# A fused two-block transformer kernel on one core: mLSTM decay matrices made during the value projection, and the first two column groups of five layer norms worked side by side

## What is computed

```
b = jnp.cumsum(lf, axis=-1)
g = b[..., -1]
a = g[..., None] - b + ic
m_loc = a.max(axis=-1)
...
dmat = b[..., :, None] - b[..., None, :] + ic[..., None, :]
dmat = jnp.where(causal, dmat, -jnp.inf)
inter = b + m_prev[..., None]
m_t = jnp.maximum(inter, dmat.max(axis=-1))
sw = jnp.exp(dmat - m_t[..., None]) * jnp.einsum('bhntk,bhnsk->bhnts', qc, kc)
s_inter = jnp.exp(inter - m_t)
```

## Time and profile before

| | us |
|---|---|
| median of 3 runs | 3019.35 (3017.84 to 3020.52) |
| profiled execution, its own time | 3024.82 |
| its span in the profile | 3023.0 |
| PE busy | 2951.9 (98%) |
| POOL busy | 2002.3 (66%) |
| DVE busy | 1487.2 (49%) |
| ACT busy | 679.4 (22%) |

### The profile page before, as it was taken

One profiled execution on the slowest core, in us unless ns is written; L12 is line 12 of the kernel. 1 busy time (PEld: TensorE's weight loads), 2 busy tenths in 40 slices (PEclk: granted clock), 3 DMA queues, 4 the chain that ended last, 5 costly groups with the idle time before them and its releaser, 6 DMA issues.

```text
span 3023.0 us, 37894 instructions
## 1 busy us (share of the span) xinstructions
PE 2951.9 (98%) x13886; PEld 2406.6 (80%) x13886; DVE 1487.2 (49%) x2621; ACT 679.4 (22%) x1500; POOL 2002.3 (66%) x2041
## 2 busy tenths in 40 slices
PE   8999999999999998999999999999999999999998
PEld 6877777788888887777888888778878888888886
DVE  7678784533324777876443322565421221324543
ACT  3265344200001336445110000000111111211000
POOL 6765455877777776444777777787766556565775
PEclk9999999999999999999999999999999999999999
DMA  4322222433334322222333333333333223222332
GB/s 145 98 85 63 64 64 73 129 96 95 94 95 127 95 90 80 58 66 66 123 92 96 97 96 99 91 91 102 97 90 105 77 84 98 84 84 77 95 96 74
DMA packets 86922, 274.37 MB, mean 91 GB/s; under 512 B 10368, under 2 KB 11008, under 8 KB 86784
## 3 DMA queue, kind: packets, MB, share of 16 engines
q1 hardware_dynamic: 85248, 270.44, 29.5%
q10 hardware_dynamic: 1536, 2.10, 0.3%
HBM read 266.21 MB, written 4.19 MB: 89 GB/s over the span
## 4 chain that ended last, share of the span: by engine, by line
PE 90%; DVE 7%; ACT 2%; issue 1%; POOL 0%; DMA 0%; DVEq 0%; SPq 0%; ACTq 0%; POOLq 0%
PE PS L498 60%; PE PS L549 14%; PE PS L778 5%; PE PS L786 3%; PE PS L824 1%; PE PS L836 1%; PE PS L1082 1%; PE PS L865 1%; PE PS L511 1%; PE PS L848 1%; PE PS L1057 0%; PE PS L1069 0%; PE PS L1054 0%; PE PS L763 0%; ACT TB L1184 0%
## 5 line engine op out<-in xcount | busy, mean ns | idle before, releaser
L468 POOL TENSOR_TENSOR WL<-RAW,WH 128x512 fp32r<-128x512 f32 (+2 forms) x538 | 798.5, 1484 | 9.8
L460 POOL TENSOR_TENSOR POOL_C<-POOL_C 128x1 f32<-128x1 f32 x538 | 126.0, 234 | 952.2 <-PE PS L498 540.8
L498 PE MATMUL PS<-XNH,WH 128*128 128x512 f32 x1752 | 692.1, 395 | 3.1 <-DVE OQK L2288 1.6
L498 PE MATMUL PS<-XNL,WH 128*128 128x512 f32 x1752 | 682.6, 390 | 0.0
L465 POOL TENSOR_TENSOR WL<-RAW,WH 128x512 fp32r<-128x512 f32 x420 | 583.5, 1389 | 35.0
L461 POOL TENSOR_SCALAR WH<-RAW 128x1024 fp32r<-128x1024 f32 (+3 forms) x538 | 533.1, 991 | 0.5 <-issue 0.5
L498 PE MATMUL PS<-XNH,WL 128*128 128x512 f32 x1752 | 433.2, 389 | 0.1
L498 PEld LDWEIGHTS PS<-XNH,WH 128*128 128x128 f32 x1752 | 328.4, 187 | 75.9 <-issue 8.2
L498 PEld LDWEIGHTS PS<-XNL,WH 128*128 128x128 f32 x1752 | 328.4, 187 | 70.7 <-issue 3.1
L498 PEld LDWEIGHTS PS<-XNH,WL 128*128 128x128 f32 x1752 | 328.0, 187 | 70.1 <-POOL WL L468 1.2
L549 PE MATMUL PS<-WH,XNH 128*128 128x512 f32 x704 | 279.3, 397 | 1.9 <-issue 1.7
(11 more groups left out here) (371 smaller groups left out, 4433.3 us busy)
## 6 DMA issues: line engine op xcount, KB each, us to landing
RAW<-w_oslot SPq DMA_DIRECT2D x56, 512.0 KB, 3.6
RAW<-w_L0ffn SPq DMA_DIRECT2D x44, 512.0 KB, 3.6
RAW<-w_L1ffn SPq DMA_DIRECT2D x44, 512.0 KB, 3.6
RAW<-w_od SPq DMA_DIRECT2D x32, 512.0 KB, 3.6
RAW<-w_L0G SPq DMA_DIRECT2D x24, 512.0 KB, 3.6
RAW<-w_L1G SPq DMA_DIRECT2D x24, 512.0 KB, 3.6
RAW<-w_epg SPq DMA_DIRECT2D x16, 512.0 KB, 3.7
RAW<-w_eug SPq DMA_DIRECT2D x16, 512.0 KB, 3.6
```

The costliest lines, as they stand in the source:

```text
L460: nc.gpsimd.tensor_tensor(POOL_C[:, 1:2], POOL_C[:, 0:1], POOL_C[:, 0:1], ALU.add)
L468: nc.gpsimd.tensor_tensor(WL[:, half, at_:w], RAW[:, slot, at_:w], WH[:, half, at_:w].bitcast(F32), ALU.subtract).then_inc(S("weights_spli ...
L498: mm = nc.tensor.matmul(bank, w[:, slot, k * cols:(k + 1) * cols], x[:, k0 + k, :], start=first and j == 0 and w is WH and x is hi, stop=l ...
```

## The change

Two things are changed, and a few orders with them.

**mLSTM.** The running sums of the gates are made in the middle of dq (`chunk_sums`, bank 4), and the four spreads during mv: before its second, third and fourth chunk and behind it, into four banks of their own. Four tiles take the place of the one `DM` (`DMS`: `DM`, an eighth of `X`, `SQA` and `DG`). VectorE does the four row maxima in a row, and the small arithmetic once for all chunks where the state doesn't force steps; it stands ahead of the low part of ckv and of the dq norms. ScalarE takes all exponentials in one go ahead of the output gate. The loop over chunks loses `maxima`, the diagonals, the exponentials and the spreads. In it, the key norm of chunk n-1 moves from the end of step n-1 to step n, behind the weighted scores. In the second layer VectorE waits for the saving of `X` to memory, since one of the tiles lies there.

**Layer norms.** At v = 1 to 5 `opening_pair` does the first two chunks together: groups k = 0 to 6 of the one and then of the other, k = 7 of both, the token sums, the low part of the first, the root's spread, the low part of the second. The residual ahead of v = 1, 3 and 5 uses other banks, and `claim` asks at these places only for banks that the next step uses. In `add_residual` `low_part` goes ahead of `add_square`.

```diff
+        DMS = (DM, X[:, 7, :], SQA[:, :], DG)
+        SPREAD_BANKS = (6, 7, 0, 5)
...
+            def opening_pair(v, banks, c, sums, roots):
+
+                def high(half, k):
+                    pe.wait_ge(S("xn_ready"), 8 * v + k + 1)
+                    for x in (XNH, XNL):
+                        nc.tensor.matmul(PS[banks[half]][:, :], WH[:, (c + half) % 2, k * P:(k + 1) * P],
+                                         x[:, k, :], start=k == 0 and x is XNH, stop=False)
+
+                for half in range(2):
+                    claim(banks[half])
+                    pe.wait_ge(S("high_ready"), c + half + 1)
+                    for k in range(KD - 1):
+                        high(half, k)
+                for half in range(2):
+                    high(half, KD - 1)
+                sum_tokens(v, sums)
+                for half in range(2):
+                    pe.wait_ge(S("weights_split"), c + half + 1)
+                    for k in range(KD):
+                        mm = nc.tensor.matmul(PS[banks[half]][:, :], WL[:, (c + half) % 2, k * P:(k + 1) * P],
+                                              XNH[:, k, :], start=False, stop=k == KD - 1)
+                    mm.then_inc(S("chunk_done"), 1)
+                    if half == 0:
+                        spread_roots(v, roots)
...
+                def spread_u(n):
+
+                    b = SPREAD_BANKS[n]
+                    claim(b)
+                    pe.wait_ge(*L("diag_ready", 4 * n + 4))
+                    nc.tensor.matmul(PS[b][:, :], ONES[:, :], DG, start=True, stop=True
+                                     ).then_inc(L("ub_ready"), 1)
+                    release[b] = L("ub_taken", n + 1)
...
+                def in_dq(q):
+                    if q == 2:
+                        chunk_sums()
+
+                def in_mv(q):
+                    if q:
+                        spread_u(q - 1)
...
+                spread_u(3)
...
-                token_group(f"L{li}mo", (1, 2, 3, 4), halfway=lambda: spread_u(0))
+                token_group(f"L{li}mo", (1, 2, 3, 4))
...
-                    if n < NT - 1:
-                        spread_u(n + 1)
...
-                residual(f"L{li}wout", 2 * li, (0, 1), [(KD, 0)], MH, ML, order=LATE_FIRST,
+                residual(f"L{li}wout", 2 * li, (2, 3), [(KD, 0)], MH, ML, order=LATE_FIRST,
...
-                            first_columns(2 * li + 1, PS[0][:, :], c, s)
-                            sum_tokens(2 * li + 1, 4)
+                            opening_pair(2 * li + 1, (0, 1), c, 4, 5)
+                            claim(2, 3)
...
+                act.wait_ge(*L("u_ready", 1))
+                diagonal(0)
                 chunk(seg("dq") + 4)
                 for n, b in enumerate((5, 6, 7, 0)):
                     run(DQR[:, n, :], PS[b][:, :], ACT.Copy, L("dq_raw"), scale=RTOK[:, n:n + 1])
+                for n in range(1, NT):
+                    diagonal(n)
...
+                act.wait_ge(*L("darg_ready", 1))
+                run(ARG, ARG, ACT.Exp, L("pex_ready"))
+                for n in range(NT):
+                    for h in range(M_HEADS):
+                        x = DMS[n][:, h * P:(h + 1) * P]
+                        run(x, x, ACT.Exp, L("pex_ready"), bias=RMAX[:, 4 * n + h:4 * n + h + 1])
...
+                    if v < 6:
+                        low_part(v, k)
                     if k > 1:
                         add_square(v, k - 1)
-                    if v < 6:
-                        low_part(v, k)
...
+                sq_tables = rope_tables(row("sq_g"), 1)
+                norm_tile(TA, 0, RSH, sq_tables, "sq")
                 dve.wait_ge(*L("bg_ready", 1))
...
+                for n in range(1, NT):
+                    norm_tile(TA, n, RSH, sq_tables, "sq")
+                if li:
+                    dve.wait_ge(S("x_saved"), 16 * KD)
+                for n in range(NT):
+                    h4 = slice(4 * n, 4 * n + 4)
+                    ub = heads(PS[SPREAD_BANKS[n]][:, :], 4)
+                    dve.wait_ge(*L("ub_ready", n + 1))
+                    V.tensor_reduce(MAXU[:, h4], ub, AX.X, ALU.max)
+                    V.tensor_tensor(heads(DMS[n], 4), ub, over(CAUSAL[:, 3 * P:], 4), ALU.add
+                                    ).then_inc(L("ub_taken"), 1)
+                    dve.wait_ge(*L("ub_taken", n + 1))
+                    ins = V.tensor_reduce(RMAX[:, h4], heads(DMS[n], 4), AX.X, ALU.max)
+                then(ins)
+                then(V.tensor_tensor(MLOC, G, MAXU, ALU.add))
+                for n in range(NT):
+                    h4 = slice(4 * n, 4 * n + 4)
+                    then(V.tensor_tensor(GM[:, h4], G[:, h4], MPREV[:, h4], ALU.add))
+                    then(V.tensor_tensor(MPREV[:, 4 * n + 4:4 * n + 8], GM[:, h4], MLOC[:, h4], ALU.max))
...
+                then(V.tensor_tensor(MX, MPREV[:, 0:16], RMAX, ALU.max))
+                V.tensor_tensor(w_loc, chunked(U), chunked(MAXU), ALU.subtract)
...
+                V.tensor_scalar(RMAX, MX, -1.0, 0.0, ALU.mult, ALU.add).then_inc(L("darg_ready"), 1)
...
                     if n:
                         total(n - 1)
-                        maxima(n)
                         state(n - 1)
```

More of the change, by code:

```diff
@@ L501, in by_columns @@
                 mm.then_inc(S("chunk_done"), 1)
-            def first_columns(v, bank, c, slot):
-                for w, xs in ((WH, (XNH, XNL)), (WL, (XNH,))):
-                    pe.wait_ge(S("high_ready" if w is WH else "weights_split"), c + 1)
-                    for k in range(KD):
-                        if w is WH:
-                            pe.wait_ge(S("xn_ready"), 8 * v + k + 1)
-                        for x in xs:
-                            mm = nc.tensor.matmul(bank, w[:, slot, k * P:(k + 1) * P], x[:, k, :],
-                                                  start=k == 0 and w is WH and x is XNH,
-                                                  stop=k == KD - 1 and w is WL)
-                mm.then_inc(S("chunk_done"), 1)
             def first_pair(v, banks, c):
@@ L552, in by_tokens, with token_group @@
                 mm.then_inc(S("chunk_done"), 1)
-            def token_group(name, banks, cols=T, k_per=2, n_k=KD, hi=XNH, lo=XNL, at=0, halfway=None):
+            def token_group(name, banks, cols=T, k_per=2, n_k=KD, hi=XNH, lo=XNL, at=0, between=None):
                 for q in range(n_k // k_per):
-                    if halfway is not None and 4 * q * k_per == 3 * n_k:
-                        halfway()
+                    if between is not None:
+                        between(q)
                     c = FIRST[name] + at + q
@@ L612, in layer @@
                         sum_tokens(2 * li, 6)
-                    if j == (1 if li else 2):
+                    if j == 2 and not li:
                         spread_roots(2 * li, 7)
@@ L627, in turn_small, with chunk_sums @@
                     release[4] = L("small_ready", 4)
-                for name, banks, sem in (("ckvq", (5, 6, 7, 0), "ckvq_raw"), ("sq", (1, 2, 3, 4), "sq_raw"),
-                                         ("dq", (5, 6, 7, 0), "dq_raw"), ("mv", (1, 2, 3, 4), "v_ready")):
-                    token_group(f"L{li}{name}", banks, halfway=turn_small if name == "ckvq" else None)
+                def chunk_sums():
+                    claim(4)
+                    pe.wait_ge(*L("lf_ready", 1))
+                    nc.tensor.matmul(PS[4][:, 0:16], TRI[:, :], LF, start=True, stop=True)
+                    nc.tensor.matmul(PS[4][:, 16:32], ONES[:, :], LF, start=True, stop=True
+                                     ).then_inc(L("bg_ready"), 1)
+                    release[4] = L("bg_taken", 1)
@@ new lines, in in_mv @@
+                def in_mv(q):
+                    if q:
+                        spread_u(q - 1)
+                for name, banks, sem, between in (("ckvq", (5, 6, 7, 0), "ckvq_raw", in_ckvq),
+                                                  ("sq", (1, 2, 3, 4), "sq_raw", None),
+                                                  ("dq", (5, 6, 7, 0), "dq_raw", in_dq),
+                                                  ("mv", (1, 2, 3, 4), "v_ready", in_mv)):
+                    token_group(f"L{li}{name}", banks, between=between)
@@ L1040, in _ @@
                 release[b0] = release[b0 + 1] = release[b0 + 2] = (S("ey_ready"), 8 + j + 1)
-            residual("eout", 4, (3, 7), [(KD, 0), (KD, 8)], EYH, EYL, ready=lambda k: (S("ey_ready"), k + 1))
-            claim(0, 1, 2, 3, 4, 5, 6, 7)
+            residual("eout", 4, (3, 5), [(KD, 0), (KD, 8)], EYH, EYL, ready=lambda k: (S("ey_ready"), k + 1))
+            claim(0, 1, 2, 4)
             def scores(s, n):
@@ L1118, in _ @@
                     c, b = FIRST[f"oslot{s}"] + q, 6 + (7 * s + q) % 2
-                    if s == 0 and q == 0:
-                        first_columns(5, PS[b][:, :], c, c % 2)
-                        sum_tokens(5, 4)
+                    if s == 0 and q < 2:
+                        if q == 0:
```

(8 more changed lines are left out.)

138 lines of the change are left out of this document (49 added, 89 removed).

## The result

| | before | after |
|---|---|---|
| median | 3019.93 us (3017.84 to 3023.21, 4 runs) | 2999.85 us (2998.97 to 3000.49, 4 runs) |
| profiled execution, its own time | 3024.82 | 2999.98 |
| its span | 3023.0 | 2998.2 |

The ratio is 0.9933, with a 95% interval of 0.992 to 0.9945: a gain of 20.1 us, where 31.6 was forecast and 2982 to 2998 was the range. The time is 11.9 us above the 2988 that was said. From profile to profile the gain is 24.8 us.

What follows compares the result with a forecast made beforehand. TensorE, busy 98% of 3023.0 us, plus its standstills was taken as the bound. Terms 17.6 + 5.1 + 1.5 + 9.4 - 2.0 = 31.6 us off 3019.35 gave 2987.8, said as 2988, range 2982 to 2998.

Steps and rivals of the forecast that it cites:

- the low clock is not in the plain runs: Rival, 15 in 100: plain runs lack the half-clock stretches, so only 26.5 us go, giving 2993 us.
- turning of the weighted scores: mLSTM loop: TensorE's waits for VectorE's product all go once the maxima leave the loop, 17.6 us.
- half-clock stretches in the loops: mLSTM loops: three stretches at the 1.2 GHz level behind TensorE's long waits go with them, 5.1 us.
- L738, L719: mLSTM loop: TensorE's waits for ScalarE go as diagonals and exponentials leave the loop; 1.5 us taken of 2.2.
- norms: Layer norms: waits for low parts, last X and the evacuation needing the root all go, 9.4 us.
- ScalarE late at the output gate: Behind mv: ScalarE's exponentials may delay the output gate; 1 us charged per layer, 2.0 together, ends 0 and 8.
- the first rival: Rival, 17 in 100: VectorE becomes the mLSTM loop's bound, held up by GpSimd; 10 us back, 2998 us.
- The 16 small operations behind mv: VectorE's small arithmetic after the last maxima, behind mv: 2.4 to 10.9 us, 6.7 taken.
- mv without a wait: During mv: the moved spreads and ScalarE's diagonals make TensorE wait nowhere, so nothing was charged.
- the product's time: Loop step 3, layer 0: VectorE's product is done by about 232.2, 2.1 us before TensorE gets there.
- The ladder: Rival, 3 in 100: in mv, diagonals and spreads wait on each other; new waits from 33.6 us make it slower.
- the empty norms: Rival, 3 in 100: at the layer norms the wait only moves, 9.4 us stay, giving 2997 us.

Runs made afterwards that it cites:

- the norm part alone: Kernel before with only the layer-norm part of the change: 3011.73 us, ratio 0.9969.
- the mLSTM part alone: Changed kernel without its layer-norm part: 3010.59 us, ratio 0.9968.
- without the subtractions: Kernel before, with GpSimd writing zeros as the low parts of the dk weights in place of subtracting: 3010.74 us, ratio 0.9967.
- the dk copies first: Changed kernel with ScalarE's copies of the second pair of dk tiles ahead of its last hidden tile: 3003.86 us, ratio 0.9947.
- the second profile of the kernel before: Kernel before, unchanged, run again: profiled execution 3022.49 us, median 3022.00 us in 12 runs.

## Why the prediction was wrong

In two steps of about equal weight: from the sum's own 2987.8 the time is 12.1 us away, 5.3 by the base and 6.8 by what is late next.

**The base: 5.3 us.** The sum was made against the profiled execution, and then "the same difference off it", 5.5 us, was taken. For the changed kernel this difference is 0.1. The removed wait was also much of what made the kernel scatter: the norm part alone, which leaves the wait in, still lies within 6.3 us (6 executions), the mLSTM part alone, which takes it out, within 2.6 (6 executions). So a gain read from one high execution is too large for the median. The rival that named this ("the low clock is not in the plain runs") had the amount, 5 us, and a reason that holds at most in part: some 3.6 of the 5.1 us are in the average plain execution, by the estimate above.

**What is late next: 6.8 us, 31.6 forecast against 24.8 from profile to profile.** By the terms:

| term | forecast | profiles |
|---|---|---|
| turning of the weighted scores | 17.6 | 17.6 |
| half-clock stretches in the loops | 5.1 | 5.1, all gone |
| L738, L719 | 1.5 | 2.2 |
| norms | 9.4 | 9.4 (alone in the median: 9.0) |
| ScalarE late at the output gate | -2.0 | 0 |
| L836, L778, not foreseen | 0 | 2.0 (1.2 and 0.8) |
| new waits: L539 6.8, L602 2.7 and 1.5 more, L729 0.5 more | 0 | -11.5 |
| sum | 31.6 | 24.8 |

The second row has its check in PE's busy time: L710, L719, L729 and L738 had 5.9 + 8.8 + 7.2 + 9.7 = 31.6 us, their successors L744, L753, L763 and L772 have 4.8 + 6.3 + 6.3 + 8.7 = 26.1. That the sum meets the 24.8 to the tenth is luck: the new waits stand in it without the prediction's 0.16 us for each, which would make it 24.5.

The failed step is the one that let the whole 17.6 us go and charged nothing for VectorE behind it, where 11.5 us of new waits came; that stood only as the first rival, at 17 in 100. The rival's mechanism is what happened, and its lateness is right: 3.5 us late said, 3.7 and 4.3 measured in the two layers. Two things in its price were wrong. It passed the lateness on only to the dk tiles' turning, 2.2 us a layer, and didn't follow it through ScalarE, whose dk copies stand behind the last hidden tile, to the bank that dv begins with, nor through the banks of state times query. And it added 3 us a layer at the output gate, which didn't come. The 16 small operations behind mv, forecast at 2.4 to 10.9 us with 6.7 taken, took 3.5, since GpSimd holds only the first (it rests from 159.54 to 162.92):

```profile
158.50 1.08 DVE L1901 TENSOR_TENSOR SMALLS<-SMALLS 128x16 f32<-128x16 f32 x1
...
161.84 0.17 DVE L1918 TENSOR_SCALAR SMALLS<-SMALLS 128x16 f32<-128x16 f32 x1
```

ScalarE then waits 4.47 us for mo before the output gate, so the charge of 2.0 falls away too. That the rival's total of 2998 is near the time is luck: its places were wrong, and it had the same base.

The key norm's move stood in the change's description and was costed at nothing. It alone is 4.5 us; put where VectorE is idle, with one root taken earlier, 10.0.

Right were the norms, the clock in the loops, mv without a wait, and the product's time: L1980 of the changed kernel is never waited for. The ladder and the empty norms are refuted.

## What to carry to other kernels

When a wait is removed, follow the engine that it hid to its next hand-over, through every engine's queue: here VectorE to ScalarE's hidden tile, to the copy behind it, to TensorE's bank. When GpSimd becomes denser with TensorE, lengthen each VectorE operation with both inputs in SBUF, however small, by the rest of the GpSimd operation that it meets: here by up to 1.1 us, from 0.15 to 1.28 and from 0.68 to 1.78. Such operations are cheap where GpSimd rests, as the sixteen behind mv show. And if a kernel's executions scatter over 8 us, price a wait from several of them, not from the one with the profile.

## What was not expected of the hardware

The hold of VectorE by GpSimd was half to two thirds of the wait in the kernel before, and a source of its scatter: the ten operations on 4 columns pass in 0.15 us each when they fall between two of GpSimd's, and up to four of them in a step take 0.9 to 1.3 us when they don't. That the scatter narrows from 8 to 3.6 us without the subtractions speaks for it too. Low-clock stretches at changing places are also in it, and the shares were not parted.

The clock doesn't follow the length of a hole alone. In the changed kernel it stays at the high level behind holes of 3.47 and 3.31 us; with the dk copies first it falls to the 1.2 GHz level behind both holes of 4.9 us; and in the second profile of the kernel before it falls behind a hole of 2.36 us, here the hole and the stretch:

```profile
207.67 0.63 PE L710 MATMUL PS<-IDENT,MS 128*128 128x128 f32 x4 [2.36 <-DVE MS L1954]
```

```profile
208.00:212.00 4.00, 3.65 (x20) 3.41 (x19) 2.96 (x8) 4.00 (x14) 1.24 (x2) 0.64 0.43 113
```

In the first profile the hole at the same place is as long, and the clock holds: the eight matmuls of L719 take 1.16 us, where they take 1.72 in the second.

```profile
209.01 0.63 PE L710 MATMUL PS<-IDENT,MS 128*128 128x128 f32 x4 [2.38 <-DVE MS L1954]
210.00 1.16 PE L719 MATMUL PS<-MS,MQK 128*128 128x129 f32 x8 [0.35 <-ACT MS L1184]
```

Two short waits in each layer were thus cheaper by 4 us in all than one with the same sum. What decides it stays open.
